# Two layers written out, second-half statistics between first-half tiles, and three units in flight at each norm

## The chip, the cores and the metric

One core of a Trainium2 chip runs the whole program once. The metric is device time in microseconds, the median of several runs.

## What is computed

Batch 1, 512 positions (T), width 1024, two layers. Cut to what matters:

```python
def _rmsnorm(x, gain):
    y = x32 * lax.rsqrt(jnp.mean(x32 * x32, axis=-1, keepdims=True) + EPS)
    return y * gain

def _modulate(h, shift, scale):
    return h * (1.0 + scale[:, None, :]) + shift[:, None, :]

for l in range(DEPTH):
    h = _modulate(_rmsnorm(x, ffn1_norm[l]), mod[:, 0, 0], mod[:, 0, 1])
    x = x + 0.5 * (1.0 + mod[:, 0, 2]) * (silu(h @ w1) * (h @ w3)) @ w2
    h = _modulate(_rmsnorm(x, mix_norm[l]), mod[:, 1, 0], mod[:, 1, 1])
    x = x + (1.0 + mod[:, 1, 2]) * hybrid_mixer(h)      # ends in mixed @ w_o
    h = _modulate(_rmsnorm(x, ffn2_norm[l]), mod[:, 2, 0], mod[:, 2, 1])
    x = x + 0.5 * (1.0 + mod[:, 2, 2]) * (silu(h @ w1) * (h @ w3)) @ w2
return _modulate(_rmsnorm(x, final_norm), fm[:, 0], fm[:, 1])
```

## The kernel before

x stays in SBUF, transposed: eight tiles `x[:, n, :]` of 128 channels by 512 positions, split by position into two halves (`HALF[0]`, `HALF[1]`) of 256 columns at every norm. Every product of a weight and an activation is three matmuls, because both are held as a rounded part (`_hi`, fp32r) and a rest (`_lo`): hi x hi, hi x lo, lo x hi (`mm3`, lines 1187 to 1189). Weights come in units of 8 x 128 x 128 (512 KB); there are ring buffers for four. For each unit SyncE loads `raw` (two buffers), ScalarE rounds it to `w_hi` (`tick`, line 436, three units ahead), GpSimd makes `w_lo` (line 406), and TensorE uses it (`unit`, `pair`). `unit_done` counts used units and frees the ring.

The five engines' programs are written by hand, each in its own order, with semaphores between them; each holds the two layers in a loop of the hardware (`Fori`), and a semaphore's target is computed from the loop's register.

A norm, numbered m, stands ahead of each block: m=-1 before the first FFN of a layer (its statistics are m=2 of the layer before), m=0 before the mixer, m=1 before the second FFN. Its steps:
- VectorE adds a finished output tile to x (`x_add`, line 828), ScalarE squares the tile (line 442), VectorE adds the square to `sqsum` (line 804). The eighth tile (n=7) comes in two halves.
- TensorE sums `sqsum` over channels (`sum_squares`, line 1244), in the down projection's last half after 10 of 22 steps k. ScalarE makes `rstd` by Ln and Exp (`norm`, lines 447 and 450).
- `h_tiles` and `h_round`: for each of eight tiles k of a half VectorE multiplies x by `rstd` (line 820), ScalarE makes `h_hi` (line 460) and the unrounded h (line 464, two buffers in turn), VectorE subtracts (line 814, `h_lo`).
- `after_norm` on TensorE (lines 1227 and 1233) uses four units on bank 0 to 3: per half, first units 0 and 1 as tiles arrive, then units 2 and 3 over all tiles.

In ScalarE's `h_round` weight ticks stand between tiles. On VectorE the second half's `x_add` and square sum follow all first-half tiles at m=0 and m=1; at the end of a layer (m=2) they come before the first-half tiles, which are at the head of the loop (lines 884 to 886, then 1115). In the mixer `w_o` gives x its tiles with one bank each, and only the eighth in two halves; then comes `sum_squares(l, 1, 0)`. After the second layer the same steps give `fin`, which ScalarE scales (line 765) and SyncE stores.

Of the kernel before, what the change touches and what calls it, by code (L numbers as in the profile page):

```python
# [98 lines left out]

class Signal:  # L100
# [5 lines left out]
    def at(self, l, k):  # L106

        assert k + self.before > 0
        return l * self.per_layer + (k + self.before)


def trunk(nc, w_units, ada_w, vecs, wf, wab, c_rows, x_in, out):
    with ExitStack() as ctx:  # L113
# [214 lines left out]
        def _(sp):  # L328
            def load_unit(l, u, idx=None):

                sp.wait_ge(unit_lo.sem, unit_lo.at(l, u - RAW + 1))
                idx = l * UNITS + u if idx is None else idx
                sp.dma_start(raw[u % RAW][:, :, :], w_units[idx]).then_inc(raw_loaded[u % RAW].sem, 16)
# [14 lines left out]
            with sp.Fori(0, DEPTH) as l:  # L348
# [22 lines left out]
            for u in range(RAW, AHEAD):  # L371
                load_unit(DEPTH, u, u)
# [9 lines left out]
        def _(gp):  # L382
# [32 lines left out]
            with gp.Fori(0, DEPTH) as l:  # L415
# [5 lines left out]
            for u in range(AHEAD):  # L421
                lo(DEPTH, u)
# [3 lines left out]
        def _(act):  # L426
            A = nc.scalar.activation

            def tick(l, u):

                n = u + AHEAD
                slot = n % RAW
                act.wait_ge(raw_loaded[slot].sem, raw_loaded[slot].at(l, 16 * (n // RAW + 1)))
                if n >= RING:
# [3 lines left out]
            def square(l, m, n, cols=slice(0, T)):  # L438

                if n >= 3:  # L440
                    act.wait_ge(sqsum_ready.sem, sqsum_ready.at(l, 8 * m + n - 2))
                A((tmp[n % 2] if n else sqsum)[:, cols], x[:, n, cols], ACT.Square).then_inc(sq_ready.sem, 1)  # L442

            def norm(l, m, h):
# [5 lines left out]
                A(rstd[:, HALF[h]], rstd[:, HALF[h]], ACT.Exp, scale=-0.5).then_inc(rstd_ready.sem, 1)  # L450

            def h_round(l, m, group, h, ticks=()):
# [3 lines left out]
                for k in range(KD):  # L456
# [5 lines left out]
                    if k >= 2:  # L462
                        act.wait_ge(hl_ready.sem, hl_ready.at(l, j - 1))
                    A(tmp[2 + k % 2][:, HALF[h]], tmp[k % 2][:, HALF[h]], ACT.Identity, bias=shift,
                      scale=scale).then_inc(hf_ready.sem, 1)
                    for after, u in ticks:
                        if k == after:
                            tick(l, u)

            def ffn(l, s):  # L470
# [14 lines left out]
                for n in range(KD - 1):  # L485
# [3 lines left out]
                    act.wait_ge(x_ready.sem, x_ready.at(l, 18 * s + n + 1))  # L489
                    square(l, 2 * s, n)  # L490
                nc.scalar.preload_act_table_set("natural_log_exp_and_others")
                act.wait_ge(x_ready.sem, x_ready.at(l, 18 * s + 8))
# [7 lines left out]
                act.wait_ge(x_ready.sem, x_ready.at(l, 18 * s + 9))  # L500
                square(l, 2 * s, KD - 1, HALF[1])
# [184 lines left out]
            square(0, -1, KD - 1, HALF[0])  # L686
            square(0, -1, KD - 1, HALF[1])
# [3 lines left out]
            with act.Fori(0, DEPTH) as l:  # L691
                h_round(l, -1, 0, 0, ((2, 0),))
# [3 lines left out]
                ffn(l, 0)  # L696
                norm(l, 0, 1)
# [40 lines left out]
                for n in range(KD):  # L738
                    tick(l, U_WO + n)
                    if n % 2 == 1 and n < KD - 1:  # L740
                        for i in (n - 1, n):
                            act.wait_ge(x_ready.sem, x_ready.at(l, 9 + i + 1))
                            square(l, 1, i)
                act.wait_ge(x_ready.sem, x_ready.at(l, 9 + 7))
                square(l, 1, KD - 2)
                nc.scalar.preload_act_table_set("natural_log_exp_and_others")
                act.wait_ge(x_ready.sem, x_ready.at(l, 9 + 8))
                square(l, 1, KD - 1, HALF[0])
                norm(l, 1, 0)
                h_round(l, 1, 2, 0, ((2, U_FFN[1]),))  # L750
                act.wait_ge(x_ready.sem, x_ready.at(l, 9 + 9))
                square(l, 1, KD - 1, HALF[1])
# [6 lines left out]
            for h in range(2):  # L759
                if h:  # L760
                    norm(DEPTH, -1, 1)
                for k in range(KD):
                    act.wait_ge(xr_ready.sem, xr_ready.at(DEPTH, 8 * h + k + 1))
                    t = fin[k // 2][:, k % 2, HALF[h]]
                    A(t, t, ACT.Identity, bias=mod[:, k:k + 1], scale=nscale[:, 0, k:k + 1]).then_inc(fin_ready.sem, 1)  # L765


        @block.vector
        def _(dve):
# [27 lines left out]
            def square_add(l, m, n, cols=slice(0, T), h=0):  # L797
# [3 lines left out]
                dve.wait_ge(sq_ready.sem, sq_ready.at(l, 9 * m + n + h + 1))  # L801
                if n > 1:
                    dve.wait_ge(sqsum_ready.sem, sqsum_ready.at(l, 8 * m + n + h - 1))
                V.tensor_tensor(sqsum[:, cols], sqsum[:, cols], tmp[n % 2][:, cols],
                                ALU.add).then_inc(sqsum_ready.sem, 1)

            def h_tiles(l, m, h):
# [4 lines left out]
                def rest(k):  # L812
                    dve.wait_ge(hf_ready.sem, hf_ready.at(l, j0 + k + 1))
                    V.tensor_tensor(h_lo[:, k, HALF[h]], tmp[2 + k % 2][:, HALF[h]],
                                    h_hi[:, k, HALF[h]].bitcast(F32), ALU.subtract).then_inc(hl_ready.sem, 1)

                for k in range(KD):
                    if k >= 2:
                        dve.wait_ge(hf_ready.sem, hf_ready.at(l, j0 + k - 1))
                    V.tensor_tensor(tmp[k % 2][:, HALF[h]], x[:, k, HALF[h]], rstd[:, HALF[h]],  # L820
                                    ALU.mult).then_inc(xr_ready.sem, 1)
                    if k:
                        rest(k - 1)
                rest(KD - 1)
# [6 lines left out]
            def ffn(l, s):  # L831
# [47 lines left out]
                dve.wait_ge(half_done.sem, half_done.at(l, 2 * s + 1))  # L879
                x_add(bank[5], KD - 1, HALF[0])  # L880
                square_add(l, 2 * s, KD - 1, HALF[0], 0)
                if s == 0:
                    h_tiles(l, 0, 0)
                dve.wait_ge(unit_done.sem, unit_done.at(l, u0 + FFN_UNITS))
                x_add(bank[7], KD - 1, HALF[1])
                square_add(l, 2 * s, KD - 1, HALF[1], 1)
# [220 lines left out]
            for h in range(2):  # L1107
                square_add(0, -1, KD - 1, HALF[h], h)
# [5 lines left out]
            with dve.Fori(0, DEPTH) as l:  # L1114
                h_tiles(l, -1, 0)
                h_tiles(l, -1, 1)
                ffn(l, 0)
                h_tiles(l, 0, 1)
# [44 lines left out]
                for n in range(KD - 1):  # L1163
                    dve.wait_ge(unit_done.sem, unit_done.at(l, U_WO + n + 1))
                    x_add(bank[WO_BANK(n)], n)
                    square_add(l, 1, n)
                dve.wait_ge(half_done.sem, half_done.at(l, 2))
                x_add(bank[WO_BANK(KD - 1)], KD - 1, HALF[0])
                square_add(l, 1, KD - 1, HALF[0], 0)
                h_tiles(l, 1, 0)  # L1170
                dve.wait_ge(unit_done.sem, unit_done.at(l, U_WO + KD))
                x_add(bank[4], KD - 1, HALF[1])
                square_add(l, 1, KD - 1, HALF[1], 1)
# [3 lines left out]
            for h in range(2):  # L1177
                dve.wait_ge(rstd_ready.sem, rstd_ready.at(DEPTH, -2 + h + 1))
                for k in range(KD):
                    V.tensor_tensor(fin[k // 2][:, k % 2, HALF[h]], x[:, k, HALF[h]], rstd[:, HALF[h]],  # L1180
                                    ALU.mult).then_inc(xr_ready.sem, 1)


        @block.tensor
        def _(pe):
# [443 lines left out]
```

## Time and profile before

| what | value |
| --- | --- |
| median of 3 runs | 2819.32 us (2815.86 to 2821.81) |
| profiled execution | 2812.3 us, its span 2810.6 us |
| instructions | 35,297 |
| mean granted clock of TensorE | 0.990 |
| busy: TensorE, VectorE, ScalarE, GpSimd | 96%, 45%, 38%, 42% |

How to read the rows: times are microseconds from the span's start unless marked ns. PE is TensorE's matmuls, PEld its weight loads, DVE VectorE, ACT ScalarE, POOL GpSimd; a "q" after an engine is its sequencer, which isn't counted as busy. `L1227` is line 1227 of the kernel. `[7.08 <-ACT h_hi L460]` is idle time of the engine before the instruction and what ended it; "issue" is idle time for which the profile shows no wait. Matmuls are pipelined: one lasts longer than the distance from its start to the next. The granted clock is 1.00 at TensorE's full 2.4 GHz and 0.5 at 1.2 GHz, here as the mean of a stretch.

### The profile page before, as it was taken

The page shows a single profiled execution, that of the slowest core. Times are in us where ns is not written, and L with a number is a line of the kernel's source. Part 1 is how long each engine was busy: PE and PEld are TensorE (multiplying, and loading weights), DVE is VectorE, ACT ScalarE, POOL GpSimd, SP SyncE. Part 2 cuts the span into 40 slices and gives each one's busy share as a digit, 9 for nine tenths or more (in the row PEclk, how much of TensorE's full clock was granted, in tenths as well). Part 3 has the DMA queues.
Part 4 walks back from the last instruction along what each step waited for, and adds up shares of the span by engine and source line. Part 5 has one row for each costly group of instructions (what it writes and reads, how often), then busy time and mean ns, then how long its engine had stood idle before and what let it go on. Part 6 is the DMA issues. An engine that isn't in the chain of part 4 may idle for free.

```text
span 2810.6 us, 35297 instructions
## 1 busy us (share of the span) xinstructions
PE 2696.0 (96%) x13124; PEld 2253.0 (80%) x13124; DVE 1258.1 (45%) x1608; ACT 1059.6 (38%) x1593; POOL 1171.8 (42%) x471
## 2 busy tenths in 40 slices
PE   3999999999999999999989999999999999999998
PEld 3888888878878878888888888888888788888886
DVE  6565337865442234411145553477545421453111
ACT  5222236644443244222242222466443432523223
POOL 2555544532223444454435554354222244355443
PEclk9999999999999999999999999999999999999999
DMA  6555532221112323533335555222122123253333
GB/s 219 210 187 203 173 116 95 88 71 60 61 54 75 98 91 127 173 92 103 97 131 191 198 189 167 89 88 91 60 60 61 46 90 98 77 187 127 103 93 97
DMA packets 91302, 325.73 MB, mean 116 GB/s; under 512 B 10096, under 2 KB 12528, under 8 KB 90864
## 3 DMA queue, kind: packets, MB, share of 16 engines
q1 hardware_dynamic: 91120, 323.35, 35.4%
q8 instruction: 108, 1.77, 0.3%
q14 instruction: 74, 0.61, 0.1%
HBM read 321.21 MB, written 2.10 MB: 115 GB/s over the span
## 4 chain that ended last, share of the span: by engine, by line
issue 54%; POOL 33%; PE 12%; POOLq 0%; ACT 0%; DVE 0%; ACTq 0%; DVEq 0%
POOL w_lo L406 32%; PE bank L1189 4%; PE bank L1187 4%; PE bank L1188 4%; POOL wab_lo L412 1%; POOLq L404 0%; ACT fin L765 0%; POOL tmp L389 0%; DVE fin L1180 0%; DVE x L828 0%; ACTq L113 0%; PE bank L1244 0%; ACT rstd L450 0%; ACT tmp L442 0%; ACT rstd L447 0%
## 5 line engine op out<-in xcount | busy, mean ns | idle before, releaser
L406 POOL TENSOR_TENSOR w_lo<-raw,w_hi 128x1024 fp32r<-128x1024 f32 x443 | 1152.4, 2611 | 1541.5 <-ACT w_hi L436 1540.9
L1187 PE MATMUL bank<-h_hi,w_hi 128*128 128x512 f32 x2240 | 876.3, 391 | 0.5
L1188 PE MATMUL bank<-h_lo,w_hi 128*128 128x512 f32 x2240 | 873.4, 390 | 0.0
L1189 PE MATMUL bank<-h_hi,w_lo 128*128 128x512 f32 x2240 | 873.1, 390 | 0.0
L436 ACT ACTIVATE w_hi<-raw 128x1024 fp32r<-128x1024 f32 x443 | 467.2, 1057 | 987.7 <-PE bank L1189 904.8
L1187 PEld LDWEIGHTS bank<-h_hi,w_hi 128*128 128x128 f32 x2240 | 421.6, 188 | 89.1 <-POOL w_lo L406 1.3
L1189 PEld LDWEIGHTS bank<-h_hi,w_lo 128*128 128x128 f32 x2240 | 421.1, 188 | 88.7
L1188 PEld LDWEIGHTS bank<-h_lo,w_hi 128*128 128x128 f32 x2240 | 421.5, 188 | 87.2
L776 DVE CUSTOM_DVE_ANT_0 ada<-ada,c_act 128x1024 f32<-128x1024 f32 x144 | 254.0, 1771 | 266.5 <-DMA ada<-ada_w 266.5
L1189 PE MATMUL bank<-g_hi,w_lo 128*128 128x512 f32 (+1 forms) x792 | 295.2, 373 | 0.0
L1188 PE MATMUL bank<-g_lo,w_hi 128*128 128x512 f32 (+1 forms) x792 | 292.4, 369 | 0.0
L1187 PE MATMUL bank<-g_hi,w_hi 128*128 128x512 f32 (+1 forms) x792 | 292.0, 369 | 0.0
L828 DVE SCALAR_TENSOR_TENSOR x<-bank,gatec,x 128x512 f32<-128x512 f32 (+1 forms) x54 | 37.2, 690 | 384.7 <-PE bank L1189 384.7
L1188 PEld LDWEIGHTS bank<-g_lo,w_hi 128*128 128x128 f32 x792 | 148.8, 188 | 30.3
L839 DVE TENSOR_TENSOR g_lo<-tmp,g_hi 128x512 fp32r<-128x512 f32 x88 | 171.6, 1954 | 0.0
L1187 PEld LDWEIGHTS bank<-g_hi,w_hi 128*128 128x128 f32 x792 | 148.6, 188 | 27.9
L1189 PEld LDWEIGHTS bank<-g_hi,w_lo 128*128 128x128 f32 x792 | 149.0, 188 | 26.7
L849 DVE TENSOR_TENSOR tmp<-tmp,bank 128x512 f32<-128x512 f32 x88 | 60.0, 681 | 224.1 <-ACT tmp L481 224.1
L1227 PE MATMUL bank<-h_hi,w_hi 128*128 128x256 f32 x384 | 107.8, 300 | 29.9 <-ACT h_hi L460 29.8
L1086 DVE TENSOR_TENSOR tmp<-tmp,bank 128x512 f32<-128x512 f32 x32 | 20.6, 684 | 194.2 <-PE bank L1189 194.2
L1227 PE MATMUL bank<-h_hi,w_lo 128*128 128x256 f32 x384 | 105.0, 293 | 0.0
L1227 PEld LDWEIGHTS bank<-h_hi,w_hi 128*128 128x128 f32 x384 | 77.9, 203 | 32.6 <-ACT h_hi L460 32.3
(208 smaller groups left out, 3057.3 us busy)
## 6 DMA issues: line engine op xcount, KB each, us to landing
raw<-w_units SPq DMA_DIRECT2D x443, 512.0 KB, 3.6
ada<-ada_w SPq DMA_DIRECT2D x144, 512.0 KB, 4.5
ada<-ada_w SPq DMA_DIRECT2D x8, 1024.0 KB, 16.5
x<-x_in SPq DMA_DIRECT2D x4, 512.0 KB, 7.3
wab_raw<-wab SPq DMA_DIRECT2D x2, 1024.0 KB, 5.7
y<-fin SPq DMA_DIRECT2D x8, 256.0 KB, 2.2
c_act<-c_rows SPq DMA_DIRECT2D x1, 512.0 KB, 3.7
vec<-vecs SPq DMA_DIRECT2D x3, 92.5 KB, 3.3
```

The lines of the kernel that those rows point to most:

```text
L406: nc.gpsimd.tensor_tensor(w_lo[s][:, :, :], raw[u % RAW][:, :, :], w_hi[s][:, :, :].bitcast(F32), ALU.subtract).then_inc(unit_lo.sem, 1)
L412: nc.gpsimd.tensor_tensor(wab_lo[c % 2][:, :, :], wab_raw[:, c, :, :], wab_hi[c % 2][:, :, :].bitcast(F32), ALU.subtract).then_inc(wabl.se ...
L436: A(w_hi[n % RING][:, :, :], raw[slot][:, :, :], ACT.Copy).then_inc(unit_hi.sem, 1)
L776: V.tensor_tensor_reduce(ada[a % 2][:, :], ada[a % 2][:, :], c_act[:, :], 1.0, 0.0, ALU.mult, ALU.add, mod[:, col:col + 1]).then_inc(ada_d ...
L828: V.scalar_tensor_tensor(out=x[:, n, cols], in0=bnk[:, cols], scalar=gatec[:, n:n + 1], in1=x[:, n, cols], op0=ALU.mult, op1=ALU.add).then ...
L839: V.tensor_tensor(g_lo[:, f, :], tmp[2 + f % 2][:, :], g_hi[:, f, :].bitcast(F32), ALU.subtract).then_inc(gl_ready.sem, 1)
L849: V.tensor_tensor(tmp[2 + f % 2][:, :], tmp[f % 2][:, :], bank[2 * (f % 2) + 1][:, :], ALU.mult).then_inc(g_ready.sem, 1)
L1086: V.tensor_tensor(sg[g][:, :], sg[g][:, :], bank[4 + 2 * (n % 2) + g][:, :], ALU.mult).then_inc(mx_step.sem, 1)
L1187: nc.tensor.matmul(o, wh, xh, start=start, stop=False, skip_group_check=True)
L1188: nc.tensor.matmul(o, wh, xl, start=False, stop=False, skip_group_check=True)
L1189: return nc.tensor.matmul(o, wl, xh, start=False, stop=stop, skip_group_check=True)
L1227: nc.tensor.matmul(bank[j][:, HALF[h]], w[(u + j) % RING][:, k, :], h_hi[:, k, HALF[h]], start=h == 0 and k == 0 and w is w_hi, stop=False ...
```

## The change

- The loop of the two layers is written out on every engine; loads, rounds and splits for units behind the second layer go.
- `rstd` goes to bank 4 (`RS`), and so does the square of tile 7's first half; the unrounded h goes to bank 5 (`HF`), one buffer per half instead of two, so that its writing waits for each `h_lo`.
- At m=0 and m=2 the second half's `x_add` (`last_half`) stands behind first-half tile 3 on VectorE, its square behind tile 3 on ScalarE, its sum behind tile 5 on VectorE; `norm(…, 1)` behind the first half. One tick moves behind `norm(…, 0)`, the other two go behind tiles 0 and 4.
- The down projection's sum of squares comes at k=6 instead of k=10.
- `after_norm`: in the first half unit 2 follows units 0 and 1 by three tiles, then unit 3 alone; in the second half units 2 and 3 follow by four.
- `w_o`: tiles 6 and 7 come in halves: first half of 6, of 7, second half of 6, of 7, in banks 4, 5, 3, 7. Their second-half adds and sums stand between first-half tiles (behind 2 and 4), the squares behind tile 2 on ScalarE; the tick of the last w_o unit behind `norm(l, 1, 0)`.

```diff
@@ sync, gpsimd, scalar, vector, tensor @@
-            with pe.Fori(0, DEPTH) as l:
+            for l in range(DEPTH):
...
@@ scalar @@
+                if l * UNITS + n >= DEPTH * UNITS:
+                    return
...
-                A((tmp[n % 2] if n else sqsum)[:, cols], x[:, n, cols], ACT.Square).then_inc(sq_ready.sem, 1)
+                dst = sqsum if n == 0 else bank[RS] if n == KD - 1 and h == 0 else tmp[n % 2]
+                A(dst[:, cols], x[:, n, cols], ACT.Square).then_inc(sq_ready.sem, 1)
...
-                A(rstd[:, HALF[h]], rstd[:, HALF[h]], ACT.Exp, scale=-0.5).then_inc(rstd_ready.sem, 1)
+                A(bank[RS][:, HALF[h]], rstd[:, HALF[h]], ACT.Exp, scale=-0.5).then_inc(rstd_ready.sem, 1)
...
-                    if k >= 2:
-                        act.wait_ge(hl_ready.sem, hl_ready.at(l, j - 1))
-                    A(tmp[2 + k % 2][:, HALF[h]], tmp[k % 2][:, HALF[h]], ACT.Identity, bias=shift,
+                    if k or h:
+                        act.wait_ge(hl_ready.sem, hl_ready.at(l, j))
+                    A(bank[HF][:, HALF[h]], tmp[k % 2][:, HALF[h]], ACT.Identity, bias=shift,
                       scale=scale).then_inc(hf_ready.sem, 1)
-                    for after, u in ticks:
-                        if k == after:
-                            tick(l, u)
+                    if k in between:
+                        between[k]()
...
-                square(l, 2 * s, KD - 1, HALF[0])
+                square(l, 2 * s, KD - 1, 0)
+                norm(l, 2 * s, 0)
                 tick(l, u0 + FFN_UNITS - 2)
-                norm(l, 2 * s, 0)
-                if s == 0:
-                    h_round(l, 0, 1, 0, ((1, u0 + FFN_UNITS - 1), (5, u0 + FFN_UNITS)))
-                else:
-                    tick(l, u0 + FFN_UNITS - 1)
...
+                    h_round(l, -1, 0, 0, {0: lambda: tick(l - 1, UNITS - 1), 3: lambda: square(l - 1, 2, KD - 1, 1),
+                                          4: lambda: tick(l, 0)})
...
+                h_round(l, 0, 1, 0, {0: lambda: tick(l, FFN_UNITS - 1), 3: lambda: square(l, 0, KD - 1, 1),
+                                     4: lambda: tick(l, FFN_UNITS)})
...
                 norm(l, 1, 0)
-                h_round(l, 1, 2, 0, ((2, U_FFN[1]),))
+                tick(l, U_WO + KD - 1)
+                h_round(l, 1, 2, 0, {2: second_squares, 4: lambda: tick(l, U_FFN[1])})
...
+                    if h == 0 and k == 3:
+                        square(DEPTH - 1, 2, KD - 1, 1)
@@ vector @@
+                    h_tiles(l, -1, 0, {3: lambda: last_half(l - 1, 1), 5: lambda: square_add(l - 1, 2, KD - 1, 1)})
                 h_tiles(l, -1, 1)
                 ffn(l, 0)
+                h_tiles(l, 0, 0, {3: lambda: last_half(l, 0), 5: lambda: square_add(l, 0, KD - 1, 1)})
...
+                h_tiles(l, 1, 0, {2: second_adds, 4: second_sums})
@@ tensor: after_norm @@
+                for k in range(KD):
+                    if k == KD - 1:
+                        sum_squares(l, m, 1)
+                    part(0, k, (0, 1))
+                    if k >= 3:
+                        part(0, k - 3, (2,))
+                for k in range(KD - 3, KD):
+                    part(0, k, (2,))
+                for k in range(KD):
+                    part(0, k, (3,))
+                for k in range(KD):
+                    part(1, k, (0, 1))
+                    if k >= 4:
+                        part(1, k - 4, (2, 3))
+                for k in range(KD - 4, KD):
+                    part(1, k, (2, 3))
@@ tensor: ffn, w_o @@
-                        if h == 1 and k == 10:
+                        if h == 1 and k == 6:
                             sum_squares(l, 2 * s, 0)
...
+                for h in range(2):
+                    for n in (KD - 2, KD - 1):
+                        sl = (U_WO + n) % RING
+                        for k in range(KD):
+                            i = mm3(bank[WO_LAST[h][n - KD + 2]][:, HALF[h]], w_hi[sl][:, k, :], w_lo[sl][:, k, :],
+                                    mx_hi[:, k, HALF[h]], mx_lo[:, k, HALF[h]], k == 0, k == KD - 1)
+                        i.then_inc((half_done, unit_done)[h].sem, 1)
                 sum_squares(l, 1, 0)
```

## Rows read from the trace of the kernel before

**Rows 1.** of the profile's page: engines' busy time, share, instructions
```profile
PE 2696.0 (96%) x13124; PEld 2253.0 (80%) x13124; DVE 1258.1 (45%) x1608; ACT 1059.6 (38%) x1593; POOL 1171.8 (42%) x471
```

**Rows 2.** stretches: length, each engine's busy us (instructions), TensorE clock, DMA share, GB/s
```profile
100.00:120.00 20.00, 20.00 (x90) 16.58 (x89) 12.77 (x15) 5.67 (x8) 9.72 (x4) 1.00 0.60 211
45.72:74.16 28.44, 26.93 (x195) 25.82 (x195) 15.77 (x35) 21.05 (x38) 7.14 (x3) 1.00 0.17 57
415.97:446.15 30.18, 26.49 (x197) 25.14 (x195) 20.33 (x48) 22.25 (x41) 8.76 (x5) 0.94 0.23 79
1042.61:1074.51 31.90, 27.60 (x196) 26.00 (x195) 15.05 (x35) 23.01 (x42) 7.12 (x3) 0.89 0.11 34
1416.33:1451.96 35.63, 27.21 (x196) 25.88 (x194) 17.44 (x39) 22.12 (x40) 7.97 (x4) 0.86 0.24 77
1793.77:1823.17 29.40, 25.14 (x196) 23.79 (x195) 20.09 (x48) 22.27 (x41) 8.49 (x5) 1.00 0.23 82
```

**Rows 3.** order of time from layer 1 to layer 2: start, length, instruction [idle before]
```profile
1412.72 0.42 ACT L450 ACTIVATE rstd<-rstd 128x256 f32<-128x256 f32 x1
...
1416.09 0.28 PE L1188 MATMUL bank<-g_lo,w_hi 128*128 128x256 f32 x1
1416.21 0.28 PE L1189 MATMUL bank<-g_hi,w_lo 128*128 128x256 f32 x1
...
1422.46 0.76 DVE L820 TENSOR_TENSOR tmp<-x,rstd 128x256 f32<-128x256 f32 x2 [4.45 <-issue]
...
1423.57 0.58 PE L1227 MATMUL bank<-h_hi,w_hi 128*128 128x256 f32 x1 [7.08 <-ACT h_hi L460]
```

**Rows 4.** order of time on ScalarE after the last matmul of the down projection
```profile
2798.56 4.04 ACT L765 ACTIVATE fin<-fin,mod,nscale 128x256 f32<-128x256 f32 x8 [0.97 <-DVE fin L1180]
2802.50 0.45 ACT L447 ACTIVATE rstd<-bank,eps_col 128x256 f32<-128x256 f32 x1
```

**Rows 5.** TensorE's queue at the loop's line 1435: duration ns min/median/max
```profile
L1435 PEldq ALU_OP  x2: 32/32/32, 1414.2 to 2794.3; - x2
L1435 PEldq COMPARE_BRANCH  x2: 83/2666/5248, 1414.3 to 2794.4; - x2
```

**Rows 6.** order of time on GpSimd, VectorE and TensorE at m=0, layer 1
```profile
416.94 2.37 POOL L406 TENSOR_TENSOR w_lo<-raw,w_hi 128x1024 fp32r<-128x1024 f32 x1 [3.42 <-ACT w_hi L436]
...
417.88 1.71 DVE L814 TENSOR_TENSOR h_lo<-tmp,h_hi 128x256 fp32r<-128x256 f32 x1 [1.17 <-ACT tmp L464]
...
419.65 0.51 PE L1233 MATMUL bank<-h_lo,w_hi 128*128 128x256 f32 x2 [1.50 <-DVE h_lo L814]
...
425.76 0.74 PE L1233 MATMUL bank<-h_lo,w_hi 128*128 128x256 f32 x2 [1.49 <-DVE h_lo L814]
```

**Rows 7.** three VectorE lines over the run: duration ns min/median/max
```profile
L814 DVE TENSOR_TENSOR h_lo<-tmp,h_hi x96: 410/426/1714, 46.2 to 2446.7; 128x256 fp32r<-128x256 f32 x96
...
L804 DVE TENSOR_TENSOR sqsum<-sqsum,tmp x56: 416/692/2477, 16.0 to 2797.7; 128x512 f32<-128x512 f32 x42, 128x256 f32<-128x256 f32 x14
...
L849 DVE TENSOR_TENSOR tmp<-tmp,bank x88: 675/680/690, 69.8 to 2674.0; 128x512 f32<-128x512 f32 x88
```

**Rows 8.** order of time on ScalarE between tiles 2 and 4 at m=1
```profile
1047.25 1.04 ACT L436 ACTIVATE w_hi<-raw 128x1024 fp32r<-128x1024 f32 x1
1048.19 0.59 ACT L460 ACTIVATE h_hi<-tmp,mod,nscale 128x256 fp32r<-128x256 f32 x1
...
1049.18 0.59 ACT L460 ACTIVATE h_hi<-tmp,mod,nscale 128x256 fp32r<-128x256 f32 x1
```

**Rows 9.** order of time on TensorE from w_o to the norm's first matmul, m=1
```profile
1042.17 0.59 PE L1244 MATMUL bank<-sqsum,ones_r 128*128 128x256 f32 x2
1044.93 0.39 PE L1227 MATMUL bank<-h_hi,w_hi 128*128 128x256 f32 x1 [2.16 <-ACT h_hi L460]
```

**Rows 10.** order of time at m=0, layer 1: last square sum and Exp of the half
```profile
408.97 0.43 DVE L804 TENSOR_TENSOR sqsum<-sqsum,tmp 128x256 f32<-128x256 f32 x1 [0.65 <-ACT tmp L442]
...
412.36 0.42 ACT L450 ACTIVATE rstd<-rstd 128x256 f32<-128x256 f32 x1
```

More of the change, by code:

```diff
@@ L97, with X_AT @@
 G0 = 2
+X_BASE = {-1: -9, 0: 0, 1: 9, 2: 19}
+SQ_BASE = {-1: -8, 0: 0, 1: 8, 2: 17}
+def X_AT(m, n, h=None):
+    if h is None:
+        return X_BASE[m] + n + 1
+    if m == 1:
+        return X_BASE[m] + 2 * h + n + 1
+    return X_BASE[m] + h + n + 1
 class Signal:
@@ L413, in wab_lo_part @@
                                         wab_hi[c % 2][:, :, :].bitcast(F32), ALU.subtract).then_inc(wabl.sem, 1)
-            with gp.Fori(0, DEPTH) as l:
+            for l in range(DEPTH):
                 for u in range(UNITS):
@@ L685, in _ @@
                 square(0, -1, n)
[L686 to L687 removed]
+            square(0, -1, KD - 1, 0)
+            square(0, -1, KD - 1, 1)
             norm(0, -1, 0)
@@ L690, in _ @@
                 tick(0, u)
-            with act.Fori(0, DEPTH) as l:
-                h_round(l, -1, 0, 0, ((2, 0),))
+            for l in range(DEPTH):
+                if l == 0:
+                    h_round(l, -1, 0, 0, {2: lambda: tick(l, 0)})
+                else:
+                    h_round(l, -1, 0, 0, {0: lambda: tick(l - 1, UNITS - 1), 3: lambda: square(l - 1, 2, KD - 1, 1),
+                                          4: lambda: tick(l, 0)})
                 norm(l, -1, 1)
@@ L823, in h_tiles @@
                         rest(k - 1)
+                    if k in between:
+                        between[k]()
                 rest(KD - 1)
@@ L1113, in _ @@
             scale_col(0, 0, V_NORM1, 0)
-            with dve.Fori(0, DEPTH) as l:
-                h_tiles(l, -1, 0)
+            for l in range(DEPTH):
+                if l == 0:
+                    h_tiles(l, -1, 0)
+                else:
+                    h_tiles(l, -1, 0, {3: lambda: last_half(l - 1, 1), 5: lambda: square_add(l - 1, 2, KD - 1, 1)})
                 h_tiles(l, -1, 1)
                 ffn(l, 0)
+                h_tiles(l, 0, 0, {3: lambda: last_half(l, 0), 5: lambda: square_add(l, 0, KD - 1, 1)})
                 h_tiles(l, 0, 1)
@@ L1179, in _ @@
                 for k in range(KD):
-                    V.tensor_tensor(fin[k // 2][:, k % 2, HALF[h]], x[:, k, HALF[h]], rstd[:, HALF[h]],
+                    V.tensor_tensor(fin[k // 2][:, k % 2, HALF[h]], x[:, k, HALF[h]], bank[RS][:, HALF[h]],
                                     ALU.mult).then_inc(xr_ready.sem, 1)
+                    if h == 0 and k == 3:
+                        last_half(DEPTH - 1, 1)
+                    if h == 0 and k == 5:
+                        square_add(DEPTH - 1, 2, KD - 1, 1)
         @block.tensor
@@ new lines, in part @@
+                def part(h, k, js):
+                    e = 16 * (m + 1) + 8 * h + k + 1
+                    if js[0] == 0:
+                        pe.wait_ge(hh_ready.sem, hh_ready.at(l, e))
+                    if h == 0 and k == 0:
+                        pe.wait_ge(unit_lo.sem, unit_lo.at(l, u + js[-1] + 1))
+                    for j in js:
+                        for w in (w_hi, w_lo):
+                            nc.tensor.matmul(bank[j][:, HALF[h]], w[(u + j) % RING][:, k, :], h_hi[:, k, HALF[h]],
+                                             start=h == 0 and k == 0 and w is w_hi, stop=False, skip_group_check=True)
+                    if js[0] == 0:
+                        pe.wait_ge(hl_ready.sem, hl_ready.at(l, e))
+                    for j in js:
+                        i = nc.tensor.matmul(bank[j][:, HALF[h]], w_hi[(u + j) % RING][:, k, :], h_lo[:, k, HALF[h]],
+                                             start=False, stop=k == KD - 1, skip_group_check=True)
+                        if h == 1 and k == KD - 1:
+                            i.then_inc(unit_done.sem, 1)
@@ L1434, in _ @@
             sum_squares(0, -1, 0)
-            with pe.Fori(0, DEPTH) as l:
+            for l in range(DEPTH):
                 ffn(l, 0)
```

162 lines of the change are left out of this document (66 added, 96 removed).

## The prediction, made before the changed kernel ran

> **What bounds the kernel now.** I read the page's first part, then the stretches of the six norms, then the order of time inside one norm of each kind. TensorE is busy for 2696.0 of 2810.6 us [rows 1]; a steady stretch at full clock has 90 matmuls of 512 columns in 20 us with its edges, so one every 0.227 us, and no idle time [rows 2]. No other engine is near that. So time can only come out of TensorE's idle and half-clock stretches, and these sit where a norm makes it wait. Each norm gives TensorE 192 matmuls of 256 columns, one per 0.12 us (those of 1416.09 and 1416.21 [rows 3]), and two matmuls of the sum of squares at some 0.22 us: 192 x 0.12 + 0.44 = 23.5 us if it never waits. [Rows 2] has the stretch from the end of the work before to the end of this block. Taking 23.5 off each:
> - start, 28.44: lost 4.9 us
> - norm 2 of a layer (m=0), 30.18 and 29.40: lost 6.7 and 5.9 us
> - norm 3 (m=1), 31.90, and the same again in the second layer: lost 8.4 us each
> - from layer 1 to layer 2, 35.63: lost 12.1 us
>
> That is 46.4 us; the tail after the last matmul of the down projection adds about another 14 us, to 2810.6, half of it under Ln and rounding that stand in line [rows 4]. The mean clock in those stretches says that part of the loss is the lower level, 1.2 GHz: 0.94, 0.89 and 0.86 against 1.00 [rows 2].
>
> **Why each is lost.** There are four causes.
> (a) VectorE has the second half's add and square sum ahead of the first half's tiles at the layer boundary. The first half's `rstd` is made at 1412.72 + 0.42, TensorE ends at 1416.33, yet the first tile is multiplied only at 1422.46, after the second half's add and square sum (lines 885 and 886) and 4.45 us of "issue", which is the jump back to the loop's head; TensorE stands for 7.08 us [rows 3]. Its own branch took 5248 ns the one time it was taken, from 1414.3 [rows 5], so it too would not have been ready before about 1419.5.
> (b) Two-operand VectorE work out of SBUF waits for GpSimd. GpSimd's `w_lo` runs 416.94 to 419.31; the `h_lo` of 417.88, 426 ns as a rule, takes 1.71 us and ends with it, and TensorE idles 1.50 us, and again 1.49 us at 425.76 [rows 6]. Over the run L814 reaches 1714 ns and L804 2477 ns, while L849, which reads one operand from a bank, stays between 675 and 690 ns in 88 instances [rows 7].
> (c) The tiles come slower than two units use them. Two ScalarE passes a tile are 0.99 us (1048.19 to 1049.18), a `tick` between them adds 0.94 us (1047.25 to 1048.19) [rows 8]. TensorE needs 6 x 0.12 = 0.72 us a tile for two units.
> (d) At m=1 the chain Ln, Exp, multiply, round follows the end of w_o in the open: sum of squares at 1042.17, first matmul at 1044.93, 2.16 us idle [rows 9].
>
> **The change, part by part.**
> *The new tile period.* `rstd` and the full-precision h now go to banks 4 and 5. The VectorE work then has one SBUF operand, so (b) goes. The h bank is single, where there were two buffers: the second pass k waits for `h_lo` k-1. A period is then the pass 0.59 [rows 8] + `h_lo` 0.426 (median of L814 [rows 7]) + two handoffs of some 0.04 = 1.10 us instead of 0.99. No row shows ScalarE writing a bank. Bounds from the nearest rows on either side: 0.42 us for that pass (the 256-column Exp in SBUF [rows 3]) and 1.04 us (the 1024-column rounding [rows 8]), so a period of 0.93 to 1.55. I take 1.10, from the pass of the same operation and size (1048.19 [rows 8], 0.59). The Trainium skill, page "ScalarE: Activation LUTs", section "Step-by-step: what each stage is for", says ScalarE writes PSUM faster than SBUF, without a figure; by that the period would be at its lower end and the sum 1 to 2 us larger. No row here can show it.
> *The third unit.* From tile 3 on TensorE has 1.08 us of work a tile (9 x 0.12), so a period of 1.10 hardly starves it; only tiles 0 to 2 can, by 1.10 - 0.72 = 0.38 us each, plus what ticks and squares put between tiles on ScalarE.
> *m=0, twice.* The sum of squares moves from k=10 to k=6 of the last half, 12 matmuls or 1.4 us earlier, to 409.8; its input is there at 409.4, so `rstd`, now at 412.78, comes at 411.4 [rows 10]. VectorE multiplies, and with the moved tick (0.94) ahead of it on ScalarE the first tile is rounded from 412.3; TensorE comes at 415.97. ScalarE starts the tiles, with its two ticks (after 0 and 4) and the square (after 3) between them, at 412.3, 414.25, 415.25, 416.35, 417.8, 419.75, 420.75 and 421.85, and each `h_lo` is done 1.6 us after that. TensorE reaches tile 4 at 419.2, wants `h_lo` of tile 5 at 420.9 and of tile 6 at 422.4: stalls of about 0.6 us in all, and 0.3 around the sum of squares. The last half's add waits on VectorE for the end of TensorE's old work; queued behind it are tiles 4 to 7, but by then TensorE has four tiles and their third units, 4 x 1.08 us, to do. Loss 0.9 instead of 6.7 and 5.9: gain 5.8 + 5.0 = 10.8.
> *Layer boundary.* The same order with no jump. First tile near 1412.9, before TensorE ends at 1416.33; the stalls sum to 0.9, with 0.3 around the sum of squares. Loss 1.2 instead of 12.1: gain 10.9. The 7.1 us idle goes whole, since the first tile now depends on nothing of the second half. What is late next is `h_lo` of tiles 5 and 6, by under 0.5 us.
> *m=1, twice.* w_o's last two tiles are split, so both first halves are summed 5.8 us before TensorE's end, but the matmul of the sum of squares still stands behind all four halves. So (d) stays: 2.3 us idle, and the tick that now follows Exp holds the first rounding back 0.3 us. TensorE then starts level with the tiles: 0.38 us at tiles 1 and 2, and 2 squares and a tick (1.8 us) in ScalarE's queue at tiles 2 and 4. Counted from tile 0, ScalarE starts the tiles at 1.0, 2.1, 3.9, 4.9, 6.95, 7.95 and 9.05; TensorE, which starts at 0.65, ends its 12.0 us of work for the half at 15.8: 3.2 us of stalls. Some 0.8 us for a stretch at half clock, and 0.3 us because 24 matmuls of 0.227 become 48 of 0.12 (5.45 to 5.76 us). 2.3 + 0.3 + 3.2 + 0.8 + 0.3 = 6.9 instead of 8.4: gain 1.5 each, 3.0 (between 0 and 5).
> *Start.* Only (b) and the third unit act, the clock is at half either way at first: gain 1.3 of 4.9.
> *Tail.* First tiles are stored while TensorE still works, and the second Ln no longer stands behind eight stores' rounding (2798.56 to 2802.50 [rows 4]). With four of them left (4 x 0.49) after the square, Ln starts at 2799.6: gain 2.9.
> *Written out.* Beside the jump, the register arithmetic ahead of waits goes; one is 32 ns on TensorE's queue [rows 5], done while the engine is at something else. I take 0; 2 us would need sixty of them in the open, and nothing speaks for a loss. Three rounds and splits for a layer that does not exist go from ScalarE and GpSimd; they lay beside TensorE: 0.
> Sum: 10.8 + 10.9 + 3.0 + 1.3 + 2.9 = 28.9 us off the profiled execution's 2812.3 us: 2783.4. The median of the runs shown is 2819.3, 7 us above the profiled one, so by it 2790.4.
>
> **The clock.** This case's rows show half clock (1.2 GHz) over part of the norm stretches, after TensorE idled; full clock is taken above for m=0 and the boundary. The Trainium skill, page "TensorE: Matmul & The Clock Gate", section "HAM oscillation — how this bites in real kernels", says idle gaps between bursts bring the clock down, so each burst begins cold. Here the stretch with the longest idle has the lowest mean (0.86) and m=0 of the second layer with 1.5 us stalls has 1.00 [rows 2], so row and page agree. Whether short stalls still do it is rival 2.
>
> **Rivals.**
> 1. The hand-over of h through one bank is slower than I take it, 1.4 us a tile. Then 8 x 0.3 = 2.4 us more in each of five first halves, 12 us; total gain 17, 2802. For: no row shows ScalarE writing a bank while VectorE reads it. Against: the same operations are sized by rows.
> 2. Stalls shrink but the low clock stays. Means of 0.94, 0.89 and 0.86 are 1.8, 3.5 and 5.0 us of clock lost in those stretches (length x (1 - mean)) [rows 2]; if 8 us of these 10 are lost while TensorE has work, 2798.
> 3. Not what it says: written-out code pauses for instructions where the loop did, 4.5 us [rows 3]; then the boundary gains only 6 and the time is 2795. Against: half of the 35,297 instructions, one pass of the loop, already run in line with no such "issue".
> 4. Slower than before: the single bank holds back also the first rounding of the next tile, so that a period is 2 x 0.587 + 0.426 + 0.15 = 1.75 us. Eight tiles are 14.0 us for 11.5 us of TensorE's work, in both halves: 5.2 us more in the first and 2.5 in the second, five norms, 38 us: 2828. It decides from a period of about 1.6. Against: `h_hi` goes to its own tile and needs only the product.
> 5. The low clock goes everywhere and m=1 gains 4 each: 2785.
>
> **How the numbers follow.** Forecast 0.66 (2785 to 2796), rival 1 0.12, rival 2 0.10, rival 3 0.04, rival 4 0.03, rival 5 0.05. The range reaches from rival 5 with 3 us for faster tiles and arithmetic saved, 2782, to rival 1, 2803; a period towards 1.55 us (2808) lies beyond it, with rival 4. A measurement of this kernel can tell about 0.2%, 5.6 us, from no change. Slower is rival 4, 0.03; the same 0.02, for gains given back elsewhere; faster 0.95.
>
> **What would show it.** No "issue" before the first multiplication at the boundary and TensorE idle under 1 us there; no `h_lo` over 0.5 us; a tile every 1.1 us; stretches of about 24.5 us at m=0, 25 at the boundary, 30 at m=1; second Ln in the tail 2.9 us earlier. The prediction falls if `h_hi` rows are more than 1.3 us apart without a tick, if the clock in m=0 stretches is below 1.00, or if idle time grows outside the norms.

## The result and the profile after

The changed kernel takes 2791.47 us (median of 4 runs, 2790.03 to 2792.80), the kernel before 2817.67 us in the same comparison: a ratio of 0.9906, 95% interval 0.9892 to 0.9920, so 26 us faster. The forecast was 2790 us. The profiled execution has a span of 2788.3 us, against 2810.6.

The stretches of the six norm blocks after, columns as in [rows 2] (start, m=0, m=1 and boundary of layer 1; m=0 and m=1 of layer 2):

```profile
44.89:73.29 28.40, 25.60 (x194) 24.97 (x195) 14.43 (x35) 21.82 (x38) 7.08 (x3) 1.00 0.15 52
415.08:439.09 24.01, 23.84 (x197) 23.50 (x196) 15.82 (x51) 21.33 (x39) 5.72 (x4) 1.00 0.30 109
1038.17:1069.67 31.50, 26.28 (x195) 24.97 (x195) 14.25 (x37) 24.73 (x44) 9.47 (x4) 0.95 0.14 46
1411.43:1437.95 26.52, 23.97 (x197) 23.48 (x195) 13.75 (x34) 19.97 (x35) 8.28 (x4) 1.00 0.35 113
1780.23:1804.21 23.98, 23.80 (x196) 23.47 (x195) 15.80 (x51) 21.34 (x39) 5.71 (x4) 1.00 0.29 109
2402.38:2433.90 31.52, 26.39 (x195) 25.05 (x195) 14.27 (x37) 24.73 (x44) 9.48 (x4) 0.95 0.15 46
```

Against [rows 2], the two at m=0 went from 30.18 and 29.40 us to 24.01 and 23.98, half a microsecond above the 23.5 of pure work, and the boundary from 35.63 to 26.52. But m=1 gained only 0.4 us each (31.90 before) and the start nothing. Whom TensorE waited for (total us, times, longest us) says why:

```profile
PE bank L1287 <- DVE sqsum L821: 27.9, 2, 26.3
PE bank L1255 <- ACT h_hi L475: 22.6, 4, 17.4
...
PE bank L1220 <- POOL w_lo L417: 9.5, 4, 2.4
...
PE bank L1260 <- DVE h_lo L831: 1.1, 6, 0.2
```

The third line is new: in the profile before TensorE never waits for `w_lo`. The last, the wait for `h_lo`, is what [rows 6] showed at 1.5 us apiece; before, it was 11.8 us in 15 waits. The new wait in order of time, at the boundary (start, length, instruction, idle before it):

```profile
1431.95 1.06 ACT L447 ACTIVATE w_hi<-raw 128x1024 fp32r<-128x1024 f32 x1 [1.66 <-PE bank L1260]
...
1433.09 4.71 POOL L417 TENSOR_TENSOR w_lo<-raw,w_hi 128x1024 fp32r<-128x1024 f32 x2 [15.40 <-ACT w_hi L447]
...
1433.39 1.05 ACT L447 ACTIVATE w_hi<-raw 128x1024 fp32r<-128x1024 f32 x1
...
1437.95 0.47 PE L1220 MATMUL bank<-h_hi,w_hi 128*128 128x512 f32 x1 [2.38 <-POOL w_lo L417]
```

ScalarE rounds the block's fifth unit once TensorE has used the first for the last time and so released its ring buffer, at 1431.95; GpSimd's two splits, 4.71 us together, end at 1437.80; TensorE, which wants both units, idles 2.38 us. The tile work itself is as it should be. Durations (ns, min/median/max) of `h_lo`, of the product with `rstd` and of ScalarE's write to bank 5:

```profile
L831 DVE TENSOR_TENSOR h_lo<-bank,h_hi x96: 416/424/426, 45.3 to 2425.0; 128x256 fp32r<-128x256 f32 x96
...
L837 DVE TENSOR_TENSOR tmp<-x,bank x96: 407/410/422, 43.7 to 2423.2; 128x256 f32<-128x256 f32 x96
...
L479 ACT ACTIVATE bank<-tmp,mod,nscale x96: 547/568/572, 44.7 to 2424.4; 128x256 f32<-128x256 f32 x96
```

No `h_lo` is over 426 ns, where L814 reached 1714 [rows 7], and the pass that writes a bank takes 568 ns.

### The profile page after: what moved, and what is told of

Its sections match the earlier page's. It is cut to its first block, busy times and chain, and to the rows that moved or that the text cites. A ratio compares the mean times of both kernels' runs of the same rounds, so it can differ in the third digit from the quotient of the medians.

```text
span 2788.3 us, 31913 instructions
## 1 busy us (share of the span) xinstructions
PE 2688.9 (96%) x13172; PEld 2250.3 (81%) x13172; DVE 1285.1 (46%) x1612; ACT 1058.8 (38%) x1592; POOL 1161.6 (42%) x468
## 4 chain that ended last, share of the span: by engine, by line
PE 85%; DVE 8%; ACT 4%; issue 1%; POOL 1%; DMA 1%; SPq 0%; ACTq 0%; DVEq 0%
PE bank L1222 26%; PE bank L1220 26%; PE bank L1221 26%; PE bank L1255 2%; PE bank L1371 1%; PE bank L1260 1%; DVE e_lo L1046 1%; DVE e_f L1074 1%; DVE e_hi L1044 1%; PE bank L1404 1%; DVE e_f L1039 1%; POOL w_lo L417 1%; DVE ada L1120 1%; DVE gt L946 1%; ACT w_hi L447 1%
## 5 line engine op out<-in xcount | busy, mean ns | idle before, releaser
L790 DVE CUSTOM_DVE_ANT_0 ada<-ada,c_act 128x1024 f32<-128x1024 f32 x144 | 287.7, 2006 | 234.0 <-DMA ada<-ada_w 234.0
L1104 DVE TENSOR_TENSOR tmp<-tmp,bank 128x512 f32<-128x512 f32 x32 | 20.6, 685 | 195.2 <-PE bank L1222 195.2
```

What stands on the lines that cost most here:

```text
L790: V.tensor_tensor_reduce(ada[a % 2][:, :], ada[a % 2][:, :], c_act[:, :], 1.0, 0.0, ALU.mult, ALU.add, mod[:, col:col + 1]).then_inc(ada_d ...
```

## The experiments

Times are medians; the ratio is to the kernel before in the same session (before: 2816.14 for e1_order, e4_sum, e5_two and e6_both, 2814.18 for e2_unroll, e7_stats and e3_sbuf, 2815.01 for after_again and e8_late, 2815.20 for e9_banks and e6_again, 2817.67 for the changed kernel). Where medians of different sessions are compared, it is by ratio.

| run | what it is | us | ratio (95%) |
| --- | --- | --- | --- |
| e2_unroll | before, written out | 2808.57 | 0.9979 (0.9970 to 0.9988) |
| e9_banks | that, and h and rstd in banks | 2802.51 | 0.9953 (0.9939 to 0.9966) |
| e7_stats | e2 and new order of statistics, w_o split | 2807.97 | 0.9981 (0.9972 to 0.9990) |
| e5_two | e7 and banks | 2789.65 | 0.9909 (0.9893 to 0.9926) |
| changed kernel | e5 and new TensorE order | 2791.47 | 0.9906 (0.9892 to 0.9920) |
| after_again | the same | 2792.66 | 0.9920 (0.9896 to 0.9945) |
| e3_sbuf | changed, without the banks | 2812.16 | 0.9990 (0.9980 to 0.9999) |
| e8_late | changed, units released later | 2813.29 | 0.9988 (0.9973 to 1.0002) |
| e1_order | changed, units released earlier | 2784.07 | 0.9887 (0.9871 to 0.9904) |
| e4_sum | changed, m=1 sum of squares earlier | 2785.15 | 0.9899 (0.9881 to 0.9916) |
| e6_both | e1 and e4 | 2777.55 | 0.9863 (0.9847 to 0.9880) |
| e6_again | the same | 2777.93 | 0.9868 (0.9854 to 0.9883) |

**e1_order: where the new wait comes from.**

```diff
                 for k in range(KD):
                     part(1, k, (0, 1))
-                    if k >= 4:
-                        part(1, k - 4, (2, 3))
-                for k in range(KD - 4, KD):
+                for k in range(KD):
                     part(1, k, (2, 3))
```

> The changed kernel with one thing undone: in a norm's second half TensorE goes over all eight tiles with units 0 and 1 first and then with units 2 and 3. My theory: the 2.37 us waits for w_lo ahead of the first full pair of units (four of them: start, layer boundary, both m=1) come from the ring, because with the units taking turns units 0 and 1 are released only 3.6 us before the block's end, where a round and two GpSimd splits take 6. Then these four waits go (9.5 us), a few tenths come back for second-half tiles that TensorE now wants a little earlier: 2782 to 2784 us. Rival: the wait is GpSimd's or ScalarE's own lateness (its queue stands behind the table load and the last tiles), then the release moves nothing and the time stays at 2790 to 2792.

2784.07 us, at the upper edge of the theory's range. The waits for `w_lo` fell from 9.5 to 2.6 us, 0.7 each, not to nothing. At the boundary:

```profile
1426.75 1.28 ACT L705 ACT_TABLE_LOAD   x1
1428.05 1.06 ACT L447 ACTIVATE w_hi<-raw 128x1024 fp32r<-128x1024 f32 x1
...
1429.19 4.89 POOL L417 TENSOR_TENSOR w_lo<-raw,w_hi 128x1024 fp32r<-128x1024 f32 x2 [13.78 <-ACT w_hi L447]
...
1434.22 0.47 PE L1220 MATMUL bank<-h_hi,w_hi 128*128 128x512 f32 x1 [0.72 <-POOL w_lo L417]
```

The pair of splits takes as long as before (4.89 us) but starts some 5 us ahead of TensorE's need. GpSimd is no slower in one kernel than in the other; what moved is the release. Units 0 and 1 are now released at 1427.75, but ScalarE starts their successors' rounding only at 1428.05, when a table load in its queue is over: that part of the 0.7 us left is the rival's, ScalarE's own queue.

**e8_late: the same cost made larger.**

```diff
                 for k in range(KD):
                     part(1, k, (0, 1))
-                    if k >= 4:
-                        part(1, k - 4, (2, 3))
-                for k in range(KD - 4, KD):
                     part(1, k, (2, 3))
```

> The changed kernel with the suspected cost made larger: in a norm's second half TensorE does units 2 and 3 of each tile at once behind units 0 and 1, so that units 0 and 1 are released 0.7 us before the block's end instead of 3.6 us. My theory (ring release): the four waits for w_lo grow from 2.37 by 2.9 to 5.2 us each, 11.5 us in all: 2802 to 2804 us. Rival (GpSimd or ScalarE late on their own account, behind tiles and table load): the waits keep their 2.4 us, and the time stays within 2 us of after_again.

> The changed kernel itself once more, beside e8_late on one chip, so that distances are taken in one session. 2790 to 2793 us, ratio to before 0.991.

The waits did exactly that, four of up to 5.2 us:

```profile
PE bank L1220 <- POOL w_lo L417: 20.8, 4, 5.2
PE bank L1220 <- DVE xa_lo L922: 5.0, 2, 4.7
...
1448.00:1456.00 8.00, 6.85 (x18) 5.45 (x19) 3.97 (x3) 3.12 (x4) 4.12 (x3) 0.57 0.75 279
```

With e1_order that is three points: units 0 and 1 released 0.7, 3.6 and 5.8 us before the block's end, waits of 5.2, 2.4 and 0.7 us. The waits of the first two differ by 2.8 us for 2.9 us of release. The third release is 2.2 us earlier still and takes only 1.7 us off the wait; the table load shown above delays ScalarE by 0.3 us of the 0.5 missing. But the kernel took 2813.29 us, 20.6 over after_again, where 11.5 were expected: the time was wrong although the mechanism was right. The two profiled executions, 23.5 us apart in span, show where the rest is. The six norm stretches together are 11.0 us longer, as expected. The FFN stretches behind the waits are 4 us longer; the boundary's wait is followed by a clock mean of 0.57 (last row above). And a 4.71 us wait for `xa_lo` stands in the mixer of layer 2, which the edit does not touch; that stretch is 8.9 us longer than in after_again (607.15 to 598.27 us).

**e5_two: what the third unit is worth.** TensorE's order of before in both halves (`part(h, k, (0, 1))` over all k, then `part(h, k, (2, 3))`), all else changed.

> The changed kernel with TensorE's order in the norm block of before in both halves: units 0 and 1 over all tiles, then units 2 and 3. Against e1_order it prices the third unit alone. My theory: the third unit fills 1.0 to 1.5 us in each of six norms, some 7 us, and costs the ring's 9.5 us: so this kernel is at 2788 to 2790 us, 6 to 7 us above e1_order and slightly below the changed kernel; no waits for w_lo. Rival: the third unit is what made the stalls at m=0 and the boundary go; then it is worth 3 us in each norm and this kernel is at 2798 or more.

2789.65 us, with 1.1 us of waits for `w_lo` where none were expected: 5.6 us above e1_order in the same session, so the third unit, with the second half's sum of squares one tile earlier, earns 5.6 us in six norms, and the new TensorE order as a whole earned nothing (0.9909 without it, 0.9906 and 0.9920 with it): the turn-taking in the second half gave back what the third unit gained.

**e4_sum and e6_both.** The sum of squares at m=1 goes ahead of w_o's last half tile.

```diff
                 for h in range(2):
                     for n in (KD - 2, KD - 1):
+                        if h == 1 and n == KD - 1:
+                            sum_squares(l, 1, 0)
                         sl = (U_WO + n) % RING
...
-                sum_squares(l, 1, 0)
```

> The changed kernel with the m=1 sum of squares issued by TensorE ahead of w_o's last half tile instead of behind it. My theory: the 2.45 us that TensorE stands at m=1 is the open chain Ln, Exp, multiply, round; 2.9 us earlier it lies under the last half tile, and the tiles come 2.9 us earlier against TensorE: 2.5 to 3.2 us in each layer, 2785 to 2787 us. Rival: TensorE is bound by the tiles' rate in that half anyway and by the second half's add, which waits for the end of w_o, so that most comes back as stalls at later tiles: 2789 to 2791 us.

> Both edits of e1_order and e4_sum in the changed kernel. My theory: they touch different waits and add up: 9 + 5.5 us off 2791.5, so 2776 to 2779 us, 1.4% under the kernel before. Rival: with the first half's tiles 2.9 us earlier at m=1 the second half's tiles are not earlier by as much, and stalls at these take 1 to 2 us a layer back: 2780 us.

> e6_both once more, on the chip of e9_banks, as the fastest version: 2776 to 2779 us, ratio 0.986 to 0.987.

2785.15 and 2777.55 us, both as the theories had them, and 2777.93 in the repeat. The m=1 stretch of e4_sum and of e6_again, and the latter's boundary:

```profile
1039.80:1068.46 28.66, 25.21 (x197) 23.76 (x195) 13.53 (x35) 22.11 (x40) 8.77 (x4) 1.00 0.16 50
1038.23:1065.29 27.06, 25.42 (x197) 23.84 (x195) 13.52 (x35) 22.10 (x40) 8.83 (x4) 1.00 0.17 55
1407.08:1432.14 25.06, 24.15 (x196) 23.52 (x195) 13.76 (x34) 19.98 (x35) 8.46 (x4) 1.00 0.35 120
```

From 31.50 us the first edit takes m=1 to 28.66 us and the second to 27.06, with the clock mean at 1.00 where it was 0.95. e6_both is 14 us faster than the changed kernel and 38 us faster than before.

**e2_unroll: the loop alone.** `for l in range(DEPTH)` for `Fori` on five engines, nothing else.

> The kernel before with only its layer loops written out, on all five engines. My theory: at the layer boundary the 4.45 us of "issue" on VectorE go, the second half's add and square sum still stand ahead of the first tile, so TensorE idles some 2.6 us instead of 7.08; everything else as before: 4 to 6 us faster, 2811 to 2813 us. Rival 1: the fetch of written-out code costs pauses of its own, the "issue" stays or turns up elsewhere, 2816 or more. Rival 2: the register arithmetic ahead of each wait was on the path in the attention stages; then idle times there shrink too and it is 8 us or more, below 2809.

5.6 us faster by its own kernel before, inside the theory's 4 to 6. In microseconds 2808.57 lies under the bound of rival 2 (2809), because the kernel before, run beside it, took only 2814.18. At the boundary:

```profile
1419.99 0.42 DVE L804 TENSOR_TENSOR sqsum<-sqsum,tmp 128x256 f32<-128x256 f32 x1 [0.48 <-ACT tmp L442]
...
1420.33 0.75 DVE L820 TENSOR_TENSOR tmp<-x,rstd 128x256 f32<-128x256 f32 x2
...
1421.59 0.35 PE L1227 MATMUL bank<-h_hi,w_hi 128*128 128x256 f32 x1 [2.60 <-ACT h_hi L460]
```

No "issue" stands before the product any more, and TensorE idles 2.60 us instead of 7.08 [rows 3]; the boundary's stretch is 4.0 us shorter (31.60 to 35.63). Neither rival shows. TensorE does have 2.5 us of "issue" ahead of the second half's sum of squares (four times, at most 0.85 us), but each ends 0.1 us behind VectorE's last addition to `sqsum` (427.40 and 427.50 at m=0), so it is the wait for that and no pause of fetching. And there is no gain from the arithmetic of the size that rival 2 asks for, 8 us.

**e7_stats, e3_sbuf, e9_banks: order of statistics and banks.** e7_stats has `rstd` and h in SBUF and TensorE's old order; e3_sbuf is the changed kernel with

```diff
-                A(bank[RS][:, HALF[h]], rstd[:, HALF[h]], ACT.Exp, scale=-0.5).then_inc(rstd_ready.sem, 1)
+                A(rstd[:, HALF[h]], rstd[:, HALF[h]], ACT.Exp, scale=-0.5).then_inc(rstd_ready.sem, 1)
...
-                    A(bank[HF][:, HALF[h]], tmp[k % 2][:, HALF[h]], ACT.Identity, bias=shift,
+                    A(tmp[2 + k % 2][:, HALF[h]], tmp[k % 2][:, HALF[h]], ACT.Identity, bias=shift,
```

and its readers and tile 7's square to match; e9_banks is e2_unroll with the opposite of the edit shown.

> Written out, with the new order of the statistics and w_o's split tiles, but rstd and h in SBUF as before and TensorE's norm block in its order of before. Beside e2_unroll it prices the order of the statistics alone, beside e5_two the banks alone. My theory: the statistics' order gains 2.6 us at the boundary, 2.9 in the tail, and under 1 us elsewhere, since the tiles still run into GpSimd's splits: 2804 to 2808 us. Then the banks are worth the largest part, 15 us or so (e5_two was 2789.65). Rival: the order of the statistics is what makes the m=0 stalls go, then this kernel is at 2795 or less and the banks are worth under 6.

> The changed kernel with rstd, the last first-half square and the unrounded h in SBUF again (two h buffers as before), all else as changed. My theory: VectorE's tile work has two SBUF operands again and waits for GpSimd's splits, 1.3 us in each of two splits a norm, and TensorE stalls for part of it although it has the third unit: 1 to 1.5 us in each of six norms, 2798 to 2801 us. Rival: the third unit covers the collisions, and two h buffers give a tile every 0.99 us instead of 1.06, so that it is no slower: 2790 to 2792.

> e2_unroll (the kernel before, written out) plus one thing: rstd and the unrounded h go to banks 4 and 5; order of statistics, w_o and TensorE's order as before. It prices the banks without the new order of the statistics (e5_two against e7_stats, some 18 us, prices them with it). Theory: the new order with its tick behind Exp puts a GpSimd split right among the first tiles (in e7_stats an h_lo of 1.74 us and a product of 2.6 us one after the other), so there the banks avoid more collisions; with the old order they avoid two a norm at 1.3 to 1.5 us, partly covered: 8 to 12 us, 2797 to 2801 us by a before of 2815 (ratio 0.994 to 0.995), and the statistics' order is then worth the rest, 8 us, once the banks are there. Rival: the banks are worth the same 18 us in either order: ratio 0.991, 2790 us, and the statistics' order is worth nothing with or without them.

None of these came out as expected. e7_stats is inside its range in microseconds, but no faster than e2_unroll (0.9981 and 0.9979), where the statistics' order was to gain some 6 us. e3_sbuf lost 20 us, neither the theory's 7 to 9 nor the rival's nothing. e9_banks is just outside its range (0.9953 for 0.994 to 0.995). The order of time in e7_stats at m=0 shows what the first two left out:

```profile
412.52 4.93 POOL L417 TENSOR_TENSOR w_lo<-raw,w_hi 128x1024 fp32r<-128x1024 f32 x2 [10.25 <-ACT w_hi L447]
...
413.45 1.74 DVE L831 TENSOR_TENSOR h_lo<-tmp,h_hi 128x256 fp32r<-128x256 f32 x1 [1.17 <-ACT tmp L479]
...
415.12 2.60 DVE L837 TENSOR_TENSOR tmp<-x,rstd 128x256 f32<-128x256 f32 x1
```

The new order puts two GpSimd splits in a row right under the first tiles: the `h_lo` of tile 0 takes 1.74 us and the next product 2.60, four microseconds in which almost nothing is delivered. In the changed kernel, here at the boundary, the same splits lie there (4.77 us from 1407.83) and the tiles run through:

```profile
1407.83 4.77 POOL L417 TENSOR_TENSOR w_lo<-raw,w_hi 128x1024 fp32r<-128x1024 f32 x2 [10.27 <-ACT w_hi L447]
...
1408.73 0.42 DVE L831 TENSOR_TENSOR h_lo<-bank,h_hi 128x256 fp32r<-128x256 f32 x1 [1.17 <-ACT bank L479]
1409.08 0.41 DVE L837 TENSOR_TENSOR tmp<-x,bank 128x256 f32<-128x256 f32 x1
```

By ratios of 2815 us the banks alone are worth 7 us, with the new order 20; the new order alone nothing, with the banks 12. These sizes hold chance matter: the traces of e3_sbuf and e9_banks have the 4.7 us wait for `xa_lo` in the mixer of layer 1, which is absent from the traces of the kernel before, of e2_unroll, e7_stats, e5_two and of the changed kernel, and e9_banks' six runs spread over 11 us. The six norm stretches of a trace (start included, each from the end of the work before to the end of the block) leave the mixers out. Their sums in us:

| | old order | new order |
| --- | --- | --- |
| in SBUF | 185.8 (e2_unroll) | 184.4 (e7_stats) |
| in banks | 174.5 (e9_banks) | 166.0 (e5_two) |

So the banks are worth 11.3 us alone and 18.4 with the new order (20.0 from e3_sbuf's 185.9 to the changed kernel's 165.9), the new order 1.4 alone and 8.5 with the banks, and each is worth some 7 us more with the other. These stretches also show where e7_stats' expected 6 us went: the boundary gained 2.4 us (31.60 to 29.20) and the tail 2.9, as said, but the two m=1 stretches lost 1.2 and 2.2 and the two mixers 1.9 and 2.9. What w_o's split and the earlier sum of squares are worth by themselves no run shows.

## Why the prediction was right

Point by point, spans of the two profiled executions:

| step | forecast gain | measured |
| --- | --- | --- |
| m=0, twice | 10.8 | 11.6 |
| layer boundary | 10.9 | 9.1 |
| m=1, twice | 3.0 | 0.8 |
| start | 1.3 | 0.9, of which 0.8 before the first matmul (44.89 us; 45.39 in e6_again) |
| tail | 2.9 | 3.1 |
| all between | 0 | -3.2 |
| sum | 28.9 | 22.3 |

- **The tile period** was to be 1.10 us. It is 1.06: `h_hi` at 1041.12 and 1042.18, without a tick between.

```profile
1041.12 0.59 ACT L475 ACTIVATE h_hi<-tmp,mod,nscale 128x256 fp32r<-128x256 f32 x1
1041.67 0.57 ACT L479 ACTIVATE bank<-tmp,mod,nscale 128x256 f32<-128x256 f32 x1
1042.18 0.58 ACT L475 ACTIVATE h_hi<-tmp,mod,nscale 128x256 fp32r<-128x256 f32 x1
```

- **m=0** was right in mechanism and size. The first tile is rounded from 411.32, 3.8 us ahead of TensorE at 415.08 (forecast: 412.3 against 415.97, 3.7 us); 0.2 us of stalls are left where 0.6 were worked out.
- **The boundary's idle time** went whole, as said. e2_unroll shows the split: 4.5 of its 7.08 us were the jump, 2.6 the order.
- **m=1** kept its 2.45 us (2.3 plus the tick's 0.3 were said), and the forecast's "so (d) stays" was confirmed by e4_sum, which removed it. Two terms were mis-sized against each other. Half clock was put at 0.8 us; from 1041.2 to 1044.7 the matmuls come one per 0.21 us instead of 0.12, which is 1.6. Stalls behind the first tile were put at 3.2 us; of the 8.0 us lost (31.50 less 23.5) 2.45, 2.37 and these 1.6 are told, so the stalls are at most 1.6.
- **What failed** is a step that the part on the third unit did not have: every reordering of TensorE's work also moves `unit_done`. I followed the tiles' arrival and not the ring's release. It cost four waits of 2.37 us, 9.5 us, at the start, the boundary and both m=1. Without it m=1 would have gained 2.8 each and the boundary 11.5. Of the signs that the prediction named, these stretches are the two that were missed: 31.5 for 30 us at m=1 and 26.5 for 25 at the boundary.
- **Why the sum still came near:** without those waits the norms and the tail would have gained 35 us, so the other terms were too low, mainly at m=1 (2.8 us each without the wait, where 1.5 were forecast) and at the start (3.3 to 1.3). That they cancel most of the 9.5 us is luck. The medians moved 26.2 us, the spans 22.3; the forecast gain of 28.9 lies above both, and 2790 was met to 1.5 us also because the kernel before had a median 1.7 us lower in this comparison (2817.67 to 2819.32).
- **Cause (b) was a larger share than I gave it**, though I did not price it apart: with the new order the banks carry some 20 us. The prediction also has `h_lo` end with the split; by [rows 6] the split ends at 419.31 and `h_lo` at 419.59. I had taken the collisions from the old order's trace. That the new order would bring more of them, if the banks were not there, I did not ask.
- **All between, -3.2 us:** the mixer of layer 1 is 2.6 us longer, that of layer 2 1.4 shorter, the rest of the last FFN 1.6 longer (343.59 us to 342.02), and the FFN behind the boundary 0.5. The 0.3 us for w_o's split is in it. The rest goes with half-clock stretches that fall elsewhere: one more in layer 1's mixer, one fewer in layer 2's, and one behind the `w_lo` wait at m=1 of layer 2 (mean 0.81 from 2431 to 2440). These I had not forecast; that the wait causes the last is argued from its place, not shown.

Rivals 1, 2 and 4 are out (period 1.06 us; means at m=0 and the boundary 1.00). Rival 3 is out by e2_unroll. Rival 5 is what e6_both became: with the first rounding out of the open m=1 gained 4.8 us, and its clock mean is 1.00.

## What to carry to other kernels

When the consumer's order is changed, follow what it releases as well as what it waits for: a ring of four units with a refill of 6 us is late by 2.4 us when the release comes 3.6 us before the next need. Price an edit in the order that it will run in, not in the old one: by the norm stretches the same bank placement was worth 11 us with one order and 18 with the other, and the new order 1.4 and 8.5. And issue the short step that opens a chain as early as its inputs allow: moving one sum of squares 2.9 us up was worth 3 us a layer.

## What the runs showed of the hardware beyond that

In the traces shown, a VectorE instruction that reads both operands from SBUF and starts under a running GpSimd split ends only 0.2 to 0.6 us behind it; with one operand in a bank none of the 192 of lines 831 and 837 did so, by the durations above. This also acts in the mixer, by chance of timing. In e8_late, from the unchanged part:

```profile
1860.61 2.40 POOL L417 TENSOR_TENSOR w_lo<-raw,w_hi 128x1024 fp32r<-128x1024 f32 x1 [0.18 <-ACT w_hi L447]
1860.74 2.81 DVE L954 TENSOR_TENSOR ya_lo<-gel,ya_hi 128x512 fp32r<-128x512 f32 x1
...
1866.08 2.36 POOL L417 TENSOR_TENSOR w_lo<-raw,w_hi 128x1024 fp32r<-128x1024 f32 x1 [3.08 <-ACT w_hi L447]
1866.27 2.71 DVE L922 TENSOR_TENSOR xa_lo<-xa,xa_hi 128x512 fp32r<-128x512 f32 x1
...
1869.04 0.79 PE L1220 MATMUL bank<-xa_hi,wab_hi 128*128 128x512 f32 x1 [4.71 <-DVE xa_lo L922]
```

It is two such meetings in one chain. `ya_lo` starts 0.13 us behind a split and takes 2.81 us instead of 0.69; `xa_lo` starts 0.19 us behind the next and takes 2.71 instead of 0.69; TensorE idles 4.71 us, where it idled 0.33 in the changed kernel. Half clock follows (mean 0.68 from 1869 to 1878), and the mixer is 8.9 us longer. In the changed kernel `ya_lo` starts at 1847.03, 0.05 us ahead of the split; it takes 0.69 us, and the split 2.90 instead of 2.40. A single meeting need not cost TensorE anything: the changed kernel's `xa_lo` at 447.47 takes 2.80 us, and TensorE does not wait for it. The same wait stands in the profiled executions of e3_sbuf and e9_banks, and in none of the kernel before, e1_order, e5_two, the changed kernel or e6_both. Runs of e8_late spread from 2804.8 to 2819.2 us, those of e6_both over less than 1 us. The two fastest of e8_late, 2804.8 and 2805.3, lie 12 us over after_again, near the 11.5 that were expected; that they are runs without this wait is not shown, since only a run of 2816.60 us has a trace. Whether this wait also makes the kernel before scatter by 10 us was not tested.
